# Sparse attention of the hybrid mixer by pairs of heads: scores, turns and outputs at every second place of a projection stream

## The chip, the core and the metric

The kernel runs on one core of one Trainium2 chip, as a single launch. The metric is the device time of one execution in microseconds; the median of three runs stands for a kernel. All data are fp32. Five instruction streams run side by side: TensorE (PE), VectorE (DVE), ScalarE (ACT), GpSimd (POOL) and SyncE (SP, which issues the DMAs).

## What is computed

The whole program is two layers of a mixed recurrent network followed by one block with a hybrid mixer and a mixture of 32 experts, for 256 tokens of width 1024. The change lies in the attention half of the hybrid mixer. Cut to what matters:

```python
DILATED_PAIRS = ((128, 1), (512, 4), (2048, 16))     # (window, dilation); 8 heads of width 64, 256 tokens

def hybrid_mixer(h, w_in, attn_norm_w, lb, hgrn_norm_w, w_out):
    proj = h @ w_in                                  # 1024 x 3584: qa ka va | qr fr ir gr
    ...
    for window, dil in DILATED_PAIRS:
        o, lse = dilated_causal_attention(qa, ka, va, window, dil)
        outs.append(o); lses.append(lse)
    wts = softmax(stack(lses), axis=0)
    o_a = einsum('nbsh,nbshd->bshd', wts, stack(outs))
    y_a = rms_norm_2(o_a, attn_norm_w)               # per head
    ...
    o_r = hgrn2_chunkwise(q_r, 1.0 - f, v_r, log(f)) # the recurrent half, 4 heads of width 128
    y_r = rms_norm_2(o_r, hgrn_norm_w) * silu(gr)
    return concatenate([y_a, y_r], axis=-1) @ w_out
```

The kernel folds the three windows into one softmax: each key gets the number of windows that contain it (0 to 3) as a factor (`cst["cnt"]`), and keys in none of them get -1e30 (`cst["neg"]`).

## The kernel before, in words

Every engine runs its stages in one fixed order: the first two layers, then `mixer2` (the hybrid mixer), then the experts (`moe_head`, `moe`). Engines wait for one another by named semaphore values: `P.mm(..., sig="at.s0")` signals, `wait_ge("at.s0")` waits, `free` says that a PSUM bank may be written again. Nothing is reordered at run time: an engine that waits holds up all that stands behind it.

In `mixer2` TensorE computes the projections `in2.*` one PSUM tile after another: a tile of `proj_p` is 16 matmuls 128x256, one of `proj_tok_p` 8 matmuls 128x512. The tiles take banks 0 to 3 in turn. The attention is a second stream *beside* this one: `att_p` is a generator, and with `P.pace = 1` each call of `P.tile` first runs it up to its next `yield`, a **step**. From the start of the stream the main tiles are

| step | 1 | 2 | 3 | 4 | 5 | 6 | 7 | 8 | 9 | 10 | 11 | 12 | 13 | 14 |
|---|---|---|---|---|---|---|---|---|---|---|---|---|---|---|
| tile after it | at.v0 | at.v1 | hg.f0 | hg.f2 | hg.q0 | hg.q2 | hg.v0 | hg.v1 | hg.g0 | hg.sc0 | hg.t0 | hg.sc1 | hg.t1 | hg.s0 |

(f, q, v, g are the gates, queries, values and output gate of the recurrent half; sc, t and s its scores, transposes and states.)

Before the change a step holds up to three things, each for another head (`k` counts the steps from 0):

- **scores** of head k: two matmuls with 64 rows (heads 2j and 2j+1 lie in rows 0 to 63 and 64 to 127 of `QA`, `KA`), into a side bank;
- **turns** of head k-1: three 128x128 transposes of the weights `PBS`, into a side bank, after `at.p{hd}`;
- **outputs** of head k-2: three matmuls from `PTB`, after ACT has copied the turned weights there (`free at.t{hd}`).

The side banks are 4 and 5, taken alternately by `side_tile`; taking one waits until its last user is free. In the code before, scores always find bank 5 (from the second on) and turns bank 4, so scores wait for DVE's reading of the scores one step earlier, and turns for ACT's copy one step earlier.

Between PE's parts, DVE scales and masks the scores (one instruction 128x384, which reads the bank), takes two maxima and negates them (`at.m`), ACT takes two exponentials (`at.e`), and DVE multiplies by the counts with a row sum (`at.p`).

DVE and ACT do their own parts of the side stream when it is **due**: `side_done(name)` records the current step, and an engine runs all side work that is due at step n just before it takes the main tile of step n. So ACT's order around step 5 is: the sigmoid parts of tile hg.f2 (`Exp`, then `Ln` and `Exp` of 512 elements), then the wait for `hg.ke` from DVE, then a `Ln` of 1024 elements, and only then, at `S.tile("hg.q0")`, the side work of step 5. Around step 7 it is: `Exp`, `Ln`, `Exp` for hg.q2, the wait for `hg.cum`, two `Exp` of 1024 elements, and then, at `S.tile("hg.v0")`, the side work of step 7. Around step 3 it is the copy of at.v1 and then the side work.

The loads of weights go through a ring of slots: SP issues the next load once PE has used the slot's former content. In the expert stage each job (two experts or four) loads units of 2 MB.

Of the kernel before, what the change touches and what calls it, by code (L numbers as in the profile page):

```python
# [9 lines left out]
ACT = mybir.ActivationFunctionType  # L10
AX = mybir.AxisListType.X
ADD, SUB, MUL, MAX, MIN = ALU.add, ALU.subtract, ALU.mult, ALU.max, ALU.min
# [609 lines left out]
def bc(ap, axis, n):  # L622

    u = ap.unsqueeze(axis)
    shape = list(u.shape)
    shape[axis] = n
    return u.to_broadcast(shape)
# [7 lines left out]
def build(nc, dram, out):  # L635
    ctx = ExitStack()
    with ctx:
# [7 lines left out]
        XS_ = sb("xs", 2 * D)  # L645
# [31 lines left out]
        cst, at = {}, 0  # L677
# [3 lines left out]
        at = sum(consts[n].shape[1] for n in list(consts)[:list(consts).index("gla")])  # L681
# [21 lines left out]
        OMU, NEG, at = {}, {}, 16  # L703
# [11 lines left out]
        def rsqrt_s(S, out, x, tmp, n):  # L715
            S.wait_ge(n + ".x")
            S.act(tmp, x, ACT.Ln)
            S.act(out, tmp, ACT.Exp, scale=-0.5)
            S.mark(n + ".e")

        def rsqrt_v(V, out, x, tmp, n):
            V.mark(n + ".x")
            V.wait_ge(n + ".e")
            V.tt(tmp, x, out, MUL)
            V.stt(tmp, tmp, -0.5, out, MUL, MUL)
            V.stt(out, tmp, 1.5, out, ADD, MUL)
# [17 lines left out]
        half64 = [slice(0, 64), slice(64, 128)]  # L744
# [1613 lines left out]
        QA, KA = MEMT[:, 0:4, :], MEMT[:, 4:8, :]  # L2358
        VA = AR.get(2, 512)
        PBS = [MX_[:, n * 384:(n + 1) * 384] for n in range(2)]  # L2360
        PTB = [MX_[:, n * 384:(n + 1) * 384] for n in range(2, 4)]
        AMX, ALS = SM[:, 124:140], SM[:, 140:156]
        OA = XS_[:, 0:1024].rearrange("p (i d) -> p i d", i=2)
        OSQ = XS_[:, 1024:2048].rearrange("p (h v) -> p h v", v=64)
        AR_, AR1, AR2 = SM[:, 156:172], SM[:, 172:188], SM[:, 188:204]
        SPLIT = ((0, slice(0, 128)), (1, slice(128, 384)))

        def att_p(P):

            oa = None  # L2370
            for k in range(10):
                if k < 8:
                    pr, j = half64[k % 2], k // 2
                    b = P.side_tile(f"at.s{k}")
                    P.wait_ge("free at.k2")
                    P.mm(b[:, 0:128], QA[pr, j, 0:128], KA[pr, j, 0:128], True, True)
                    P.mm(b[:, 128:384], QA[pr, j, 128:256], KA[pr, j, :], True, True, sig=f"at.s{k}")
                    P.side_done(f"at.s{k}")
                if 1 <= k < 9:
                    hd = k - 1  # L2380
                    b = P.side_tile(f"at.t{hd}")
                    P.wait_ge(f"at.p{hd}")
                    for q in range(3):
                        P.tr(b[:, q * 128:(q + 1) * 128], PBS[hd % 2][:, q * 128:(q + 1) * 128], ident,
                             sig=f"at.t{hd}" if q == 2 else None)
                    P.side_done(f"at.t{hd}")
                if k >= 2:
                    hd = k - 2
                    if hd == 0:
                        oa = [P.occupy(f"at.o{i}", 6 + i) for i in range(2)]  # L2390
                    vs = slice(hd * 64, hd * 64 + 64)
                    ptb = PTB[hd % 2]
                    P.wait_ge(f"free at.t{hd}", "free at.v1")
                    P.mm(oa[0][:, vs], ptb[:, 0:128], VA[:, 0, vs], True, True)
                    P.mm(oa[1][:, vs], ptb[:, 128:256], VA[:, 0, vs], True, False)
                    P.mm(oa[1][:, vs], ptb[:, 256:384], VA[:, 1, vs], False, True, sig=f"at.h{hd}")
                yield True
            for _ in range(2):
                yield True
            P.m.put("due at.sq", P.steps + 1)  # L2400
            yield True
            P.m.put("due at.o", P.steps + 1)
            for _ in range(2):
                yield True
            for i in range(2):
                b = P.side_tile(f"at.y{i}")
                P.wait_ge("at.on")
                for c in range(4):
                    P.tr(b[:, c * 128:(c + 1) * 128], OA[:, i, c * 128:(c + 1) * 128], ident,
                         sig=f"at.y{i}" if c == 3 else None)  # L2410
                P.side_done(f"at.y{i}")
            yield True

        def att_v(V):
            for hd in range(8):
                yield V.due_at(f"at.s{hd}")
                pb = PBS[hd % 2]
                b = V.got(f"at.s{hd}")
                if hd > 1:
                    V.wait_ge(f"at.t{hd - 2}")  # L2420
                V.stt(pb, b[:, 0:384], 0.125, cst["neg"], MUL, ADD)
                V.free(f"at.s{hd}")
                for i, s in SPLIT:
                    m = AMX[:, i * 8 + hd:i * 8 + hd + 1]
                    V.reduce(m, pb[:, s], MAX)
                    V.ts(m, m, -1.0, None, MUL, None)
                V.mark(f"at.m{hd}")
                V.wait_ge(f"at.e{hd}")
                for i, s in SPLIT:
                    V.stt(pb[:, s], pb[:, s], 1.0, cst["cnt"][:, s], MUL, MUL, accum=ALS[:, i * 8 + hd:i * 8 + hd + 1])  # L2430
                V.mark(f"at.p{hd}")
            yield V.due_at("at.o")
            V.recip(ALS, ALS)
            V.tt(AR2, ALS, ALS, MUL)
            V.wait_ge("at.sq")
            V.reduce(AR1, OSQ, ADD)
            V.tt(AR1, AR1, AR2, MUL)
            V.ts(AR1, AR1, 1.0 / 64, EPS, MUL, ADD)
            rsqrt_v(V, AR_, AR1, AR2, "at")
            V.tt(AR_, AR_, ALS, MUL)  # L2440
            for i in range(2):
                V.tt(OA[:, i, :].rearrange("p (h v) -> p h v", h=8), V.banks[6 + i].rearrange("p (h v) -> p h v", h=8),
                     bc(AR_[:, i * 8:i * 8 + 8], 2, 64), MUL)
                V.free(f"at.o{i}")
            V.mark("at.on")
            for i in range(2):
                yield V.due_at(f"at.y{i}")
                b = V.got(f"at.y{i}")
                V.tt(MIX[:, 0:4, i * 128:(i + 1) * 128], b.rearrange("p (c t) -> p c t", c=4),
                     bc(COL[:, coff["ang"]:coff["ang"] + 4], 2, 128), MUL)  # L2450
                V.free(f"at.y{i}")

        def att_s(S):
            for hd in range(8):
                yield S.due_at(f"at.s{hd}")
                pb = PBS[hd % 2]
                S.wait_ge(f"at.m{hd}")
                for i, s in SPLIT:
                    S.act(pb[:, s], pb[:, s], ACT.Exp, bias=AMX[:, i * 8 + hd:i * 8 + hd + 1])
                S.mark(f"at.e{hd}")  # L2460
                yield S.due_at(f"at.t{hd}")
                b = S.got(f"at.t{hd}")
                S.copy(PTB[hd % 2], b[:, 0:384])
                S.free(f"at.t{hd}")
            yield S.due_at("at.sq")
            S.wait_ge("at.h7")
            for i in range(2):
                S.act(OSQ[:, i * 8:i * 8 + 8, :], S.banks[6 + i].rearrange("p (h v) -> p h v", h=8), ACT.Square)
            S.mark("at.sq")
            yield S.due_at("at.o")  # L2470
            rsqrt_s(S, AR_, AR1, AR2, "at")
# [10 lines left out]
        def mixer2_p(P):  # L2482
# [4 lines left out]
            proj_p(P, "in2.0", "at.q", xn="m2")  # L2487
            proj_p(P, "in2.1", "at.k")
            P.beside(att_p(P))
            P.pace = 1  # L2490
            proj_tok_p(P, "in2.2", "at.v")
# [64 lines left out]
        def mixer2_s(S):  # L2556
# [12 lines left out]
            for n, dst in (("at.q", QA), ("at.k", KA)):  # L2569
                for j in (0, 2):  # L2570
                    b = S.tile(f"{n}{j}")
                    S.copy(dst[:, j:j + 2, :], pair(b))
                    S.free(f"{n}{j}")
            S.beside(att_s(S))
            S.wait_ge("hg.l")
            S.act(z0, z0, ACT.Exp)
# [59 lines left out]
        def mixer2_v(V):  # L2636
# [4 lines left out]
            root_v(V, "fin", out=RB1)  # L2641
            scaled_v(V, HT, HT, gain_of("final_g"), "fin", r=RB1, sig="h")
            V.beside(att_v(V))
            l0, l1 = COL[:, coff["lb"]:coff["lb"] + 4], COL[:, coff["lb"] + 4:coff["lb"] + 8]
            V.tt(lb, l0, l1, MAX)
# [108 lines left out]
        cnt, cum, st = NOV[:, 0, :], NOV[:, 1, :], NOV[:, 2, :]  # L2754
# [836 lines left out]
```

## Time and profile before

| | |
|---|---|
| median of 3 runs | 2265.56 us (2265.2 to 2265.84) |
| the profiled execution | 2268.09 us, span of its trace 2266.2 us |
| PE busy | 2127.8 us, 94% of the span |
| DVE, ACT, POOL busy | 619.3, 370.2, 125.3 us |
| DMA | 587.54 MB, mean 259 GB/s |
| mean granted TensorE clock | 0.974 of full |

The three medians agree within 0.6 us. The profile's times below are us from the start of the span. The side stream runs from 1144.7 (first scores) to about 1229. A matmul in fp32 is recorded as two instructions, a transpose as one; the busy time of PE overlaps from one instruction to the next, so the cost of a group is read from its start to the start of the next group.

### The profile page before, as it was taken

The numbers are of one execution on the slowest core, as the hardware profiler recorded it, in microseconds if no ns is written. First come the engines' busy times: TensorE is split into PE (matmuls) and PEld (weight loads), VectorE is DVE, ScalarE is ACT, GpSimd is POOL, SyncE is SP. The second block draws the span as 40 slices with busy tenths as digits, with TensorE's granted clock in tenths as the row PEclk, the third lists the DMA queues.
The fourth block names the chain that finished last, engine by engine and source line by source line (L and its number), as shares of the span: only waits on it lengthen the run. The fifth ranks groups of instructions, "written<-read, shape, count | busy, mean of one in ns | idle before, by whom it ended". The sixth has DMA issues, their size and how long they took to land.

```text
span 2266.2 us, 25809 instructions
## 1 busy us (share of the span) xinstructions
PE 2127.8 (94%) x10764; PEld 1413.8 (62%) x10764; DVE 619.3 (27%) x1229; ACT 370.2 (16%) x672; POOL 125.3 (6%) x186
## 2 busy tenths in 40 slices
PE   9999999999999999999999999996789999999765
PEld 6887788888888888888877753332334333433222
DVE  4344432334454224336225321000001010100001
ACT  4321122100014222000222320100001000001000
POOL 0113300000000000000000010100000000001000
PEclk9999999999999999999999999998889999999888
DMA  6321053444632445336533459999999999999997
GB/s 252 112 75 38 2 208 115 151 161 156 237 149 101 159 149 223 149 140 271 235 146 112 188 222 402 428 427 427 427 427 420 425 428 427 426 392 428 427 428 281
DMA packets 44427, 587.54 MB, mean 259 GB/s; under 512 B 5344, under 2 KB 5616, under 8 KB 9104
## 3 DMA queue, kind: packets, MB, share of 16 engines
q1 hardware_dynamic: 44304, 585.82, 63.8%
q8 instruction: 87, 1.43, 0.3%
q14 instruction: 36, 0.29, 0.0%
HBM read 584.75 MB, written 1.05 MB: 258 GB/s over the span
## 4 chain that ended last, share of the span: by engine, by line
PE 73%; DMA 24%; DVE 1%; ACT 1%; issue 1%; SPq 0%; PEld 0%; DVEq 0%; ACTq 0%; PEldq 0%
PE pb L410 72%; DMA kv<-in_gu 7%; DMA ring<-in_gu 6%; DMA ring<-in_dne 6%; DMA kv<-in_dne 2%; DMA arena<-in_dne 2%; PE pb L420 1%; DMA arena<-in_gu 1%; DVE arena L327 1%; ACT arena L371 0%; DVE arena L312 0%; DMA ht<-in_x 0%; DVE arena L321 0%; ACT arena L377 0%; DMA ring<-in_dn 0%
## 5 line engine op out<-in xcount | busy, mean ns | idle before, releaser
L410 PE MATMUL pb<-arena,ring 128*128 128x256 f32 (+1 forms) x2816 | 614.1, 380 | 4.9 <-ACT arena L371 2.0
L410 PEld LDWEIGHTS pb<-arena,ring 128*128 128x128 f32 (+1 forms) x2816 | 522.6, 188 | 89.4 <-issue 8.7
L410 PE MATMUL pb<-arena 128*128 128x256 f32 (+12 forms) x2644 | 491.3, 383 | 34.0 <-DMA ring<-in_dne 16.6
L410 PEld LDWEIGHTS pb<-arena 128*128 128x128 f32 (+5 forms) x2644 | 317.7, 168 | 194.1 <-issue 158.9
L410 PE MATMUL pb<-arena,cst 128*64 128x512 f32 (+6 forms) x1032 | 338.0, 617 | 58.6 <-DMA kv<-in_gu 40.8
L410 PE MATMUL pb<-ring,cst 128*64 128x512 f32 (+2 forms) x800 | 341.3, 628 | 0.0
L410 PEld LDWEIGHTS pb<-arena,cst 128*64 128x64 f32 (+4 forms) x1032 | 104.6, 140 | 265.4 <-issue 262.8
L410 PE MATMUL pb<-ring,arena 128*64 128x512 f32 (+2 forms) x480 | 192.1, 619 | 7.3 <-DMA arena<-in_dne 7.3
L377 ACT ACTIVATE arena<-pb 128x512 f32<-128x512 f32 (+4 forms) x123 | 68.7, 559 | 550.8 <-PE pb L420 420.4
L319 DVE TENSOR_SCALAR arena<-pb 128x512 f32<-128x512 f32 x30 | 20.8, 692 | 466.6 <-PE pb L410 466.6
L410 PEld LDWEIGHTS pb<-ring,cst 128*64 128x64 f32 (+2 forms) x800 | 100.0, 140 | 67.6 <-issue 67.6
L371 ACT ACTIVATE arena<-arena 128x512 f32<-128x512 f32 (+5 forms) x155 | 90.2, 582 | 300.6 <-DVE arena L327 271.1
L410 PE MATMUL pb<-kv,cst 128*64 128x512 f32 (+2 forms) x288 | 135.7, 627 | 0.0
L312 DVE TENSOR_TENSOR arena<-pb,arena 128x512 f32<-128x512 f32 (+5 forms) x114 | 60.7, 533 | 239.0 <-PE pb L410 230.4
L321 DVE TENSOR_SCALAR arena<-pb 128x512 f32<-128x512 f32 x30 | 20.7, 691 | 338.0 <-PE pb L410 338.0
L410 PEld LDWEIGHTS pb<-ring,arena 128*64 128x64 f32 (+2 forms) x480 | 62.3, 146 | 62.7 <-issue 62.7
L410 PE MATMUL pb<-arena,kv 128*128 128x256 f32 (+1 forms) x448 | 95.9, 380 | 1.2 <-ACT arena L377 1.2
L312 DVE TENSOR_TENSOR arena<-arena 128x512 f32<-128x512 f32 (+6 forms) x138 | 81.8, 593 | 39.4 <-ACT arena L371 29.0
L410 PEld LDWEIGHTS pb<-arena,kv 128*128 128x128 f32 (+1 forms) x448 | 80.8, 186 | 13.9 <-ACT arena L377 1.6
L377 ACT ACTIVATE memt<-pb 128x512 f32<-128x512 f32 x36 | 21.5, 597 | 377.7 <-PE pb L410 377.5
L327 DVE SCALAR_TENSOR_TENSOR arena<-arena 128x512 f32<-128x512 f32 (+4 forms) x94 | 67.2, 715 | 18.9 <-ACT arena L371 11.0
L410 PEld LDWEIGHTS pb<-arena,xs 128*128 128x128 f32 (+2 forms) x540 | 63.2, 190 | 10.1 <-issue 8.7
(145 smaller groups left out, 1472.3 us busy)
## 6 DMA issues: line engine op xcount, KB each, us to landing
arena<-in_gu SPq DMA_DIRECT2D x60, 2048.0 KB, 18.6
ring<-in_gu SPq DMA_DIRECT2D x50, 2048.0 KB, 19.4
arena<-in_dne SPq DMA_DIRECT2D x33, 2048.0 KB, 19.4
ring<-in_dne SPq DMA_DIRECT2D x21, 2048.0 KB, 19.4
kv<-in_gu SPq DMA_DIRECT2D x18, 2048.0 KB, 19.4
ring<-in_up SPq DMA_DIRECT2D x13, 2048.0 KB, 7.8
ring<-in_wkv SPq DMA_DIRECT2D x8, 2048.0 KB, 7.8
ring<-in_dn SPq DMA_DIRECT2D x8, 2048.0 KB, 7.6
```

Source lines behind the costliest of these rows:

```text
L312: self.e.tensor_tensor(out, a, b, op).then_inc(self.sem, 1)
L319: self.e.tensor_scalar(out, a, s1, None, op0).then_inc(self.sem, 1)
L321: self.e.tensor_scalar(out, a, s1, s2, op0, op1).then_inc(self.sem, 1)
L327: self.e.scalar_tensor_tensor(out, a, s, b, op0, op1, accum_out=accum).then_inc(self.sem, 1)
L371: self.e.activation(out, a, func, bias=bias, scale=scale, accum_out=accum).then_inc(self.sem, 1)
L377: self.e.activation(out, a, ACT.Copy).then_inc(self.sem, 1)
L410: r = self.e.matmul(out, lhsT, rhs, start=start, stop=stop, skip_group_check=True)
L420: r = self.e.transpose(out, a, ident)
```

## The change

The head-by-head pipeline becomes one of pairs. Scores of both heads of a pair are issued together, alternating between the two row halves; the turns of a pair are issued together, and so are its outputs. All this stands at the odd steps only: scores of pair j at step 2j+1, turns of pair j at step 2j+3 ahead of the scores of pair j+1, outputs of pair j at step 2j+5 between the two. The outputs of the last pair stand at step 10. DVE and ACT do both heads of a pair together, and `PTB` has four buffers where it had two.

```diff
+        PTB += [XS_[:, 1024 + n * 384:1408 + n * 384] for n in range(2)]
...
-            for k in range(10):
-                if k < 8:
-                    pr, j = half64[k % 2], k // 2
-                    b = P.side_tile(f"at.s{k}")
-                    P.wait_ge("free at.k2")
+            def scores(j):
+                bs = [P.side_tile(f"at.s{2 * j + n}") for n in range(2)]
+                P.wait_ge("free at.k2")
+                for b, pr in zip(bs, half64):
                     P.mm(b[:, 0:128], QA[pr, j, 0:128], KA[pr, j, 0:128], True, True)
-                    P.mm(b[:, 128:384], QA[pr, j, 128:256], KA[pr, j, :], True, True, sig=f"at.s{k}")
-                    P.side_done(f"at.s{k}")
-                if 1 <= k < 9:
-                    hd = k - 1
+                for n, (b, pr) in enumerate(zip(bs, half64)):
+                    P.mm(b[:, 128:384], QA[pr, j, 128:256], KA[pr, j, :], True, True, sig=f"at.s{2 * j + n}")
+                P.side_done(f"at.s{2 * j + 1}")
+
+            def turns(j):
+                for hd in (2 * j, 2 * j + 1):
                     b = P.side_tile(f"at.t{hd}")
                     P.wait_ge(f"at.p{hd}")
...
-                if k >= 2:
-                    hd = k - 2
...
+            def heads(j):
+                if j == 0:
+                    oa.update({i: P.occupy(f"at.o{i}", 6 + i) for i in range(2)})
+                for hd in (2 * j, 2 * j + 1):
                     vs = slice(hd * 64, hd * 64 + 64)
-                    ptb = PTB[hd % 2]
+                    ptb = PTB[hd % 4]
                     P.wait_ge(f"free at.t{hd}", "free at.v1")
...
+            for j in range(5):
+                if j >= 1:
+                    turns(j - 1)
+                if j >= 2:
+                    heads(j - 2)
+                if j < 4:
+                    scores(j)
+                yield True
+                if j == 4:
+                    heads(3)
                 yield True
...
         def att_s(S):
-            for hd in range(8):
-                yield S.due_at(f"at.s{hd}")
...
+            for j in range(4):
+                heads = (2 * j, 2 * j + 1)
+                yield S.due_at(f"at.s{2 * j + 1}")
+                for hd in heads:
+                    S.wait_ge(f"at.m{hd}")
...
+                yield S.due_at(f"at.t{2 * j + 1}")
+                for hd in heads:
+                    b = S.got(f"at.t{hd}")
+                    S.copy(PTB[hd % 4], b[:, 0:384])
+                    S.free(f"at.t{hd}")
```

In `att_v` the waits and instructions are the same, with the masks and maxima of both heads first and the two multiplications of each head after them.

## Rows read from the trace of the kernel before

**Rows 1.** The page: the chain that ended last, by engine.

```profile
PE 73%; DMA 24%; DVE 1%; ACT 1%; issue 1%; SPq 0%; PEld 0%; DVEq 0%; ACTq 0%; PEldq 0%
```

**Rows 2.** The chain in order of time, around 1370: start, us, what.

```profile
1370.23 7.04 PE pb L410 x32
1377.66 17.38 DMA kv<-in_gu
```

**Rows 3.** Busy time by stretch: PE, PEld, DVE, ACT, POOL, granted clock, DMA share, GB/s.

```profile
1310.00:1378.00 68.00, 65.71 (x330) 29.48 (x332) 12.45 (x37) 8.40 (x15) 8.48 (x17) 0.97 0.70 275
1378.00:1591.00 213.00, 181.70 (x896) 69.84 (x892) 21.19 (x38) 19.26 (x33) 15.23 (x32) 0.94 1.01 427
```

**Rows 4.** Timeline of PE at step 7: scores, turns, outputs, next tile.

```profile
1196.41 0.92 PE L410 MATMUL pb<-memt 64*128 64x128 f32 x4
1197.26 0.55 PE L420 MATMUL pb<-cst,arena 128*128 128x128 f32 x3
1197.64 0.78 PE L410 MATMUL pb<-arena 128*128 128x64 f32 x6
1198.26 7.09 PE L410 MATMUL pb<-ring,arena 128*128 128x512 f32 x16
```

**Rows 5.** Timeline of PE: matmuls in alternate row halves, and what follows them.

```profile
1087.71 2.00 PE L410 MATMUL pb<-arena 64*128 64x256 f32 x16
1089.64 4.58 PE L410 MATMUL pb<-arena,ring 128*128 128x256 f32 x20
```

**Rows 6.** Timeline of ACT at step 2: tile at.v0, then the copy of a turn.

```profile
1152.69 0.60 ACT L377 ACTIVATE arena<-pb 128x512 f32<-128x512 f32 x1 [4.00 <-PE pb L410]
1154.02 0.49 ACT L377 ACTIVATE arena<-pb 128x384 f32<-128x384 f32 x1 [0.73 <-PE pb L420]
```

**Rows 7.** Timeline of all engines at step 2, DVE: the first and the last work on one head.

```profile
1153.54 0.56 DVE L327 SCALAR_TENSOR_TENSOR arena<-pb,cst 128x384 f32<-128x384 f32 x1 [4.05 <-PE pb L410]
...
1156.59 0.42 DVE L327 SCALAR_TENSOR_TENSOR arena<-arena,cst 128x256 f32<-128x256 f32 x1
```

**Rows 8.** Timeline of all engines at step 5, PE and ACT.

```profile
1178.59 0.92 PE L410 MATMUL pb<-memt 64*128 64x128 f32 x4
...
1178.70 0.60 ACT L371 ACTIVATE arena<-pb 128x512 f32<-128x512 f32 x1 [2.84 <-PE pb L410]
...
1182.02 1.06 ACT L371 ACTIVATE arena<-arena 128x1024 f32<-128x1024 f32 x1 [1.39 <-DVE arena L321]
...
1183.16 0.49 ACT L377 ACTIVATE arena<-pb 128x384 f32<-128x384 f32 x1
```

**Rows 9.** Timeline of ACT at step 7.

```profile
1197.14 3.47 ACT L371 ACTIVATE arena<-arena 128x512 f32<-128x512 f32 x4
1200.70 0.49 ACT L377 ACTIVATE arena<-pb 128x384 f32<-128x384 f32 x1
```

**Rows 10.** Timeline of PE at steps 10 to 14: outputs and hg.sc0, hg.t0, hg.s0.

```profile
1221.96 1.72 PE L410 MATMUL pb<-arena 128*128 128x64 f32 x14
1223.52 0.60 PE L420 MATMUL pb<-cst,arena 128*128 128x128 f32 x4
...
1226.86 1.12 PE L410 MATMUL pb<-arena 32*128 32x128 f32 x8 [0.97 <-DVE arena L312]
```

**Rows 11.** Timeline of ACT at steps 11 to 13: copies of hg.t0 and hg.t1.

```profile
1224.17 0.60 ACT L377 ACTIVATE arena<-pb 128x512 f32<-128x512 f32 x1
...
1226.12 0.60 ACT L377 ACTIVATE arena<-pb 128x512 f32<-128x512 f32 x1
```

**Rows 12.** Timeline of PE at tile hg.f0, a whole tile of a projection.

```profile
1162.63 7.12 PE L410 MATMUL pb<-arena,ring 128*128 128x256 f32 x32
```

**Rows 13.** Busy time by stretch, as in Rows 3: short stretches, earlier stages.

```profile
701.40:704.90 3.50, 2.41 (x11) 1.51 (x9) 0.91 (x3) 3.12 (x6) 0.00 (x0) 0.99 0.00 0
704.90:708.30 3.40, 3.07 (x8) 2.61 (x9) 3.26 (x5) 1.30 (x4) 0.00 (x0) 0.51 0.00 0
1111.10:1114.50 3.40, 2.18 (x11) 1.57 (x9) 2.65 (x6) 0.86 (x3) 0.00 (x0) 1.00 1.00 429
```

More of the change, by code:

```diff
@@ L2368, in att_p @@
         def att_p(P):
-            oa = None
-            for k in range(10):
-                if k < 8:
-                    pr, j = half64[k % 2], k // 2
-                    b = P.side_tile(f"at.s{k}")
-                    P.wait_ge("free at.k2")
-                    P.mm(b[:, 0:128], QA[pr, j, 0:128], KA[pr, j, 0:128], True, True)
-                    P.mm(b[:, 128:384], QA[pr, j, 128:256], KA[pr, j, :], True, True, sig=f"at.s{k}")
-                    P.side_done(f"at.s{k}")
-                if 1 <= k < 9:
-                    hd = k - 1
+            oa = {}
+            def scores(j):
+                bs = [P.side_tile(f"at.s{2 * j + n}") for n in range(2)]
+                P.wait_ge("free at.k2")
+                for b, pr in zip(bs, half64):
+                    P.mm(b[:, 0:128], QA[pr, j, 0:128], KA[pr, j, 0:128], True, True)
+                for n, (b, pr) in enumerate(zip(bs, half64)):
[3 more added lines that the diff above has]
+                for hd in (2 * j, 2 * j + 1):
                     b = P.side_tile(f"at.t{hd}")
@@ L2385, in att_p @@
                              sig=f"at.t{hd}" if q == 2 else None)
-                    P.side_done(f"at.t{hd}")
-                if k >= 2:
-                    hd = k - 2
-                    if hd == 0:
-                        oa = [P.occupy(f"at.o{i}", 6 + i) for i in range(2)]
+                P.side_done(f"at.t{2 * j + 1}")
+            def heads(j):
+                if j == 0:
+                    oa.update({i: P.occupy(f"at.o{i}", 6 + i) for i in range(2)})
+                for hd in (2 * j, 2 * j + 1):
                     vs = slice(hd * 64, hd * 64 + 64)
-                    ptb = PTB[hd % 2]
+                    ptb = PTB[hd % 4]
                     P.wait_ge(f"free at.t{hd}", "free at.v1")
@@ L2415, in att_v @@
             for hd in range(8):
-                yield V.due_at(f"at.s{hd}")
                 pb = PBS[hd % 2]
+                if hd % 2 == 0:
+                    yield V.due_at(f"at.s{hd + 1}")
                 b = V.got(f"at.s{hd}")
@@ L2427, in att_v @@
                 V.mark(f"at.m{hd}")
[L2428 to L2431, printed above, removed]
+                if hd % 2 == 0:
+                    continue
+                for h1 in (hd - 1, hd):
+                    V.wait_ge(f"at.e{h1}")
+                    for i, s in SPLIT:
+                        pb = PBS[h1 % 2][:, s]
+                        V.stt(pb, pb, 1.0, cst["cnt"][:, s], MUL, MUL, accum=ALS[:, i * 8 + h1:i * 8 + h1 + 1])
+                    V.mark(f"at.p{h1}")
             yield V.due_at("at.o")
@@ L2453, in att_s @@
         def att_s(S):
-            for hd in range(8):
-                yield S.due_at(f"at.s{hd}")
[L2456 to L2464, printed above, removed]
+            for j in range(4):
[3 more added lines that the diff above has]
+                    S.wait_ge(f"at.m{hd}")
+                    for i, s in SPLIT:
+                        pb = PBS[hd % 2][:, s]
+                        S.act(pb, pb, ACT.Exp, bias=AMX[:, i * 8 + hd:i * 8 + hd + 1])
+                    S.mark(f"at.e{hd}")
+                yield S.due_at(f"at.t{2 * j + 1}")
[3 more added lines that the diff above has]
+                    S.free(f"at.t{hd}")
             yield S.due_at("at.sq")
```

## The prediction

> **What bounds the kernel now.** I read the chain that ended last first: 73% of it is PE, 24% DMA [rows 1]. In order of time it is almost only PE up to 1377, and at 1377.66 it passes to loads of expert weights that follow one another [rows 2]. The busy times by stretch say the same: from 1378 on the DMA engines are fully busy (share 1.01, 427 GB/s), in the 68 us before only 0.70 of the time [rows 3]. The changed place, 1144 to 1229, lies in the PE part. Here PE never waits for the side stream: a step with all three parts is followed at once by its projection tile [rows 4]. So each microsecond that PE gains or loses here moves all that comes after. That holds for the DMA part too: its loads are issued when PE gives a slot back, and no load in the 0.70 stretch fills the engines, so the stream of loads starts as much later as PE does. I count 1:1.
>
> **What PE's work costs, before and after.** From start to start at step 7 [rows 4]: scores of one head 0.85 us (1196.41 to 1197.26), turns 0.38, outputs 0.62; 1.85 a head, 14.8 us for eight.
>
> Scores of a pair: four matmuls, recorded as eight instructions, four with 128 columns and four with 256. The trace has no such group, but it has 16 instructions 64x256 in alternate row halves: 1.93 us from start to start, 0.121 each [rows 5], where a 128-row instruction with 256 columns takes 7.12/32 = 0.2225 [rows 12]. So the halves do overlap, to nearly twice the rate. A single head's 0.85 against 2 x 0.11 + 2 x 0.2225 = 0.67 leaves 0.18 for filling and changing over. For the pair: low bound 4 x 0.06 + 4 x 0.121 = 0.72, all at double rate with no edge; high bound twice 0.85 = 1.70, no overlap and nothing saved. I take 1.10: the 256-column ones at 0.121, the 128-column ones near their full 0.11 since each still loads 128 columns of weights, and an edge of 0.18. Turns of a pair: 2 x 0.33 + 0.05 = 0.71. Outputs: 12 instructions at 0.62/6, 1.24. Together 3.05 a pair, 12.2 for four: **2.6 us less** than 14.8. With the bounds of the scores it is 4.1 less to 0.2 less.
>
> The Trainium skill (TensorE: Matmul & The Clock Gate, Part 3, The mechanism) says that matmuls in different row groups run at the same time, and the halves above agree in part (1.8 times the rate). By that rule alone a pair's scores would take one head's 0.85, and the sum below would be 1.0 us smaller.
>
> **The wait that the new order puts in.** The side banks are two. `scores(j)` takes both before its first matmul, and the users before it are the two turns of the *same* step. So PE, standing at step 3, 5 or 7, must wait until ACT has copied both turns out; behind it stand the scores and the next projection tile. Before, the copy had a whole tile (7.12 us, [rows 12]) of cover; now it has only the outputs in between (1.24 at steps 5 and 7, nothing at step 3). And ACT does the copies only after its work on the main tile that has just ended. Let T be the end of the main tile ahead of the step, which is also the start of the step.
>
> - *Step 3.* ACT copies at.v1 first (0.60, starting 0.11 after T, as [rows 6]: 1152.69 against 1152.58). The turns' results come 0.55 after their start; copies of 0.49 from T+0.73, T+1.25, done at T+1.74. With 0.14 for the signal PE starts the scores at T+1.88, without the wait at T+0.71: **1.17**.
> - *Step 5.* T = 1178.59 in the old trace. ACT does tile hg.f2 (0.60 and 1.29), waits for DVE (`hg.ke`; 1.39 idle), does its `Ln` of 1.06, and starts the one copy of this step at 1183.16, T+4.57 [rows 8]. None of what stands ahead of it depends on the new order, so the two copies end at T+5.56 and the scores start at T+5.70. PE has turns and outputs until T+1.95: **3.75**.
> - *Step 7.* T = 1196.41. ACT runs 3.47 us in four `Ln` and `Exp` with no gap, so `hg.cum` isn't late, and the copy starts at 1200.70, T+4.29 [rows 9]. Two copies end at T+5.28, scores at T+5.42: **3.47**. DVE's scan ahead of `hg.cum` follows tile hg.q0; it still has the whole tile hg.q2 (7.12) and ACT's work on that (1.9) ahead of the wait, only the side work of step 6 (1.85) is gone from between.
>
> Sum of the waits **8.4 us**. Their bounds: nothing (rival 4), and 9.9 with one more ACT instruction of 0.49 ahead of each two copies.
>
> Other waits stay covered. From the first DVE instruction to the last one head takes 3.5 us [rows 7], a pair some 5.5; between scores and turns of a pair lie two tiles, 14 us. Steps 9 and 10 have no scores, so their turns and outputs wait for nothing.
>
> *Step 10* now has outputs of two heads, 0.62 more. The idle 0.97 ahead of hg.s0 [rows 10] looks like cover, but ACT's copy of hg.t0 starts at 1224.17, right after PE's transposes end (1223.52 + 0.60), and the copy of hg.t1 ends at 1226.72, 0.14 ahead of hg.s0 [rows 11]. So this 0.62, which is inside the 12.2, is not hidden. I count it in full.
>
> PE's sum: -2.6 + 8.4 = **+5.8 us**.
>
> **The clock.** An idle stretch can also cost speed. At 701.4 to 704.9 PE was busy 2.41 of 3.5 us, a good part of it in matmuls of 4 rows, and at 704.9 to 708.3 it was granted 0.51, the 1.2 GHz level, with 8 matmuls where 3.40/0.2225 = 15 would fit; that costs 1.7 us. With 2.18 of 3.40 busy at 1111 it kept 1.00, the 2.4 GHz level [rows 13]. The two waits of 3.5 to 3.75 leave PE far emptier than either. I expect a fall after each, of 0.8 to 1.7 us, part of it lying in the wait itself: **+2.4** for both, bounds 0 and 3.5. The wait of 1.17 costs no clock.
>
> The Trainium skill (same page, Part 1, What's actually happening) says the clock is throttled by default and only activity releases it, which speaks against this change; the row at 704.9 agrees.
>
> Total +5.8 + 2.4 = **+8.2**: 2265.56 + 8.2 = 2273.8 us, 0.36% slower. The profiled execution was 2268.09 (span 2266.2), 2.5 above the median; such an execution of the changed kernel would be near 2276.3, its span 2274.4.
>
> **The rivals.**
>
> 1. *Waits and clock, as forecast*: 2273.8, range 2271.5 to 2276. Chance 0.55.
> 2. *Waits without the clock*: the turns and outputs around the waits keep it at 2.4 GHz, as at 1111. 2265.56 + 5.8 = 2271.4. Chance 0.2.
> 3. *The row halves don't overlap*, so the change doesn't do what it says: one bank after another, 1.33 + 0.18 = 1.5 to 1.7 for a pair, that is 1.6 to 2.4 more. 2273.8 + 2 = 2275.8. For it: the two heads start with their 128-column matmuls, which no row shows alternating; against it: [rows 5]. Chance 0.1.
> 4. *The copies come in time* (the other side): ACT takes the copies before its work on the finished tile, at T+0.7 at steps 5 and 7. Then the outputs cover them but for 0.1 to 0.6. It decides once the copies end before T+1.8, against T+5.56 by my reading of the order. Only the gain is left, less about 1 us at step 3: 2265.56 - 1.5 = 2264.1, no difference that can be measured. Chance 0.08.
> 5. *The delay is swallowed later*: 8 us less idle for PE in the expert stage, where it has 31 of 213 us idle [rows 3], since the DMA stream sets the end. It would need loads that are issued at the old time whatever PE does. 2265.6 to 2268. Chance 0.07.
>
> **How the numbers follow.** What a measurement of this kernel can tell from no change is about 0.2%, 4.5 us, so the border is at 2270.1. Rival 1 and 3 are above it, rival 2 mostly (its own spread is about 2 us; I give 0.15 of its 0.2), 4 and 5 within. Slower 0.81, same 0.17, faster 0.02. The range of 8 in 10 takes in rival 2 and 3, leaving out 4, 5 and the ends: 2268.5 to 2277.5.
>
> **What the profile after would show.** PE idle ahead of its memt matmuls (the scores) three times, about 1.2, 3.7 and 3.5 us, released by ACT's copies of 128x384; nothing of this ahead of the turns. Groups of eight memt instructions of about 1.1 us from start to start, four times. ACT copies in twos. Steps 2, 4, 6 and 8 without any side work. A granted clock of about 0.5 for some 3 us after step 5 and after step 7. The chain passing from PE to DMA near 1386 instead of 1377.66. It would make me wrong if ACT's copies stood ahead of its main tile's work, if the release of a bank came otherwise than through those copies, or if the DMA stream started at its old time.

## The result and the profile after

The changed kernel takes 2278.91 us (median of 4 runs, 2277.48 to 2280.86) against 2265.70 beside it: 1.0059 times, 95% interval 1.0041 to 1.0076, so 13.2 us slower. The forecast was 2273.8 with a range up to 2277.5. The direction was right, the size and the range were not. One execution of a later kernel (four side banks, late outputs, split biases) took 2674.55 us at a mean granted clock of 0.84; it does not count in that kernel's ratio, and without it the median is 2262.99 instead of 2263.24.

The profiled execution of the changed kernel took 2278.09 us, its span is 2276.3. PE around the side stream, from the timeline of the kernel after (start, us, engine and operation, in brackets the idle time before and what ended it):

```profile
1142.14 0.93 PE L410 MATMUL pb<-memt 64*128 64x128 f32 x8 [0.78 <-ACT memt L377]
...
1156.83 0.82 PE L420 MATMUL pb<-cst,arena 128*128 128x128 f32 x6
1158.94 0.93 PE L410 MATMUL pb<-memt 64*128 64x128 f32 x8 [1.29 <-ACT arena L377]
...
1173.71 0.82 PE L420 MATMUL pb<-cst,arena 128*128 128x128 f32 x6
1174.37 1.45 PE L410 MATMUL pb<-arena 128*128 128x64 f32 x12
1179.59 1.02 PE L410 MATMUL pb<-memt 64*128 64x128 f32 x8 [3.77 <-ACT xs L377]
1180.54 15.63 PE L410 MATMUL pb<-arena,ring 128*128 128x256 f32 x64
...
1196.66 1.45 PE L410 MATMUL pb<-arena,xs 128*128 128x64 f32 x12
1201.66 1.66 PE L410 MATMUL pb<-memt 64*128 64x128 f32 x8 [3.56 <-ACT arena L377]
1203.25 16.14 PE L410 MATMUL pb<-ring,arena 128*128 128x512 f32 x32
...
1233.69 1.12 PE L410 MATMUL pb<-arena 32*128 32x128 f32 x8 [1.40 <-ACT arena L377]
1234.75 8.86 PE L410 MATMUL pb<-arena,kv 128*128 128x256 f32 x32
```

The `memt` rows are the scores, now eight instructions for a pair. The three new waits stand ahead of them and nowhere else, 1.29, 3.77 and 3.56 us; before the change PE had none here [rows 4]. ACT just ahead of the second one, in the timeline of ACT after, shows what it waited for: the `Ln` of 1024 elements behind `hg.ke`, then the two copies:

```profile
1177.22 1.06 ACT L371 ACTIVATE arena<-arena 128x1024 f32<-128x1024 f32 x1 [1.39 <-DVE arena L321]
1178.37 1.07 ACT L377 ACTIVATE xs<-pb 128x384 f32<-128x384 f32 x2
```

The copies start 4.66 us after the tile's end at 1173.71 (before 4.57, [rows 8]). Behind the long waits the two tiles between two steps, 14.1 us at full clock, take 15.6 and 16.1. Busy time by stretch of the kernel after (PE, PEld, DVE, ACT, POOL, granted clock, DMA share, GB/s):

```profile
1176.00:1179.60 3.60, 0.01 (x2) 0.04 (x2) 1.12 (x3) 2.04 (x3) 0.00 (x0) 1.00 0.92 387
1180.30:1183.70 3.40, 3.40 (x10) 2.54 (x9) 2.78 (x9) 0.91 (x2) 0.00 (x0) 0.50 0.41 149
...
1200.80:1207.60 6.80, 5.93 (x13) 2.81 (x14) 3.77 (x13) 2.23 (x6) 0.00 (x0) 0.50 0.31 129
1234.90:1238.30 3.40, 3.40 (x9) 2.65 (x10) 2.56 (x9) 0.43 (x2) 0.00 (x0) 0.50 0.02 5
1347.50:1350.90 3.40, 3.40 (x10) 0.77 (x8) 0.00 (x0) 0.00 (x0) 0.00 (x0) 0.51 1.02 439
```

So the clock is at its 1.2 GHz level (a **fall** in what follows) behind step 5, for twice as long behind step 7, once behind hg.s0 (ahead of which PE idled 1.40 us), and in the expert stage at 1347.5. The chain passes to the DMA stream 8.5 us later than in the first profile of before [rows 2]:

```profile
1378.73 7.04 PE pb L410 x32
...
1386.17 17.28 DMA kv<-in_gu
```

The forecast had 1386 for this, but the hit is luck: the two profiles do not start the side stream at the same time, and from the first scores on the change costs 11.1 us up to this point (244.0 against 233.0).

Profiles of one kernel differ in the stages ahead of and behind the change, by where the clock falls. The first profile of before fell at 128.0 and 704.9, the profile after at 1112.0 instead, and the first began its scores 2.6 us later. At 1112.0 to 1115.4 the profile after was granted 0.50, and so was the second profile of before at 1112.7 to 1116.1, both behind 2.00 us of idle. Behind the same idle, which lies in the third line of [rows 13], the first profile of before kept 1.00. The instructions there are the same, so they alone do not decide whether a fall comes. So I compare stretches, from the starts in the PE timelines (e0 is the first job of the expert stage, and 32x512 its matmuls with 32 rows and 512 columns; the DMA stream begins where the chain passes to DMA):

| kernel | first scores | to hg.s0 | hg.s0 to first 32x512 of e0 | that to the DMA stream | from there to the span's end |
|---|---|---|---|---|---|
| before, two profiles | 1144.7, 1142.6 | 82.2, 82.2 | 92.7, 92.7 | 58.1, 56.4 | 888.5, 889.8 |
| after, two profiles | 1142.1, 1144.7 | 91.5, 91.5 | 94.4, 94.3 | 58.1, 58.1 | 890.1, 894.8 |

Up to hg.s0 the change costs 9.4 us, both times; 1.7 are added right behind it, both times; the rest of the 13 lies further behind. That rest is badly known: the interval of the ratio makes the whole 9.3 to 17.2 us, and the execution of the second profile of after took 2285.24 us, 4.7 above its median.

### The profile page after: what moved, and what is told of

It is laid out like the page before. It is cut to its first block, busy times and chain, and to the rows that moved or that the text cites. A ratio compares the mean times of both kernels' runs of the same rounds, so it can differ in the third digit from the quotient of the medians.

```text
span 2276.3 us, 25805 instructions
## 1 busy us (share of the span) xinstructions
PE 2130.8 (94%) x10764; PEld 1415.4 (62%) x10764; DVE 619.5 (27%) x1229; ACT 370.2 (16%) x672; POOL 125.2 (6%) x186
## 4 chain that ended last, share of the span: by engine, by line
PE 71%; DMA 25%; ACT 2%; DVE 1%; issue 0%; SPq 0%; ACTq 0%; DVEq 0%
PE pb L410 70%; DMA ring<-in_gu 8%; DMA kv<-in_gu 8%; DMA ring<-in_dne 5%; DMA kv<-in_dne 3%; DMA arena<-in_gu 1%; DMA arena<-in_dne 1%; PE pb L420 1%; ACT arena L371 1%; DVE arena L327 1%; ACT arena L377 0%; DVE arena L321 0%; DMA ht<-in_x 0%; ACT xs L371 0%; DVE arena L312 0%
## 5 line engine op out<-in xcount | busy, mean ns | idle before, releaser
L410 PE MATMUL pb<-arena 128*128 128x256 f32 (+12 forms) x2620 | 486.4, 383 | 31.5 <-DMA ring<-in_dne 17.3
L410 PEld LDWEIGHTS pb<-arena 128*128 128x128 f32 (+5 forms) x2620 | 312.9, 167 | 192.7 <-issue 157.4
```

What stands on the lines that cost most here:

```text
L410: r = self.e.matmul(out, lhsT, rhs, start=start, stop=stop, skip_group_check=True)
```

## The experiments

Each was timed in five rounds beside the kernel before (medians of 2265.4 to 2266.8); ratios are to that, with 95% intervals. Spare matmuls are 128x256 with a result that nobody uses, about 0.44 us each.

### Four side banks

```diff
-        k = self.second[self.j % 2]
+        k = self.second[self.j % len(self.second)]
...
             P.pace = 1
+            P.main, P.second = [0, 1], [2, 3, 4, 5]
...
             proj_tok_p(P, "in2.5", "hg.v")
+            P.main, P.second, P.j = [0, 1, 2, 3], [4, 5], 0
```

> The changed kernel with four side banks (2 to 5) and two main banks (0, 1) during steps 1 to 8, so that scores no longer take the banks of the turns of the same step. Theory A (the wait for ACT's copies of the turns and the clock falls behind it are the whole loss): no wait ahead of the scores at steps 3, 5 and 7, no fall of the granted clock near them, PE's side work 3.6 us less than before the change (0.86 instead of 1.70 for the scores of a pair in the profile after), so about 2262, 3 to 4 us faster than the kernel before. Theory B (the loss comes from DVE and ACT doing two heads at a time, which makes the main tiles late): the time stays near 2279. Theory C (two main banks are too few, a new wait of projection tiles for their banks takes the place): idle of PE ahead of 128x256 or 128x512 projection matmuls, and a time between 2264 and 2275.

2265.17 us, ratio 0.9995 (0.9986 to 1.0003). What PE waited for from 1140 to 1240, in this kernel:

```profile
PE pb L410 <- ACT arena L377: 1.4, 1, 1.4
PE pb L410 <- ACT memt L377: 0.8, 1, 0.8
```

The three waits are gone and no main tile waits for a bank. From scores to hg.s0 it is 78.21 us, 3.95 less than before the change and 13.3 less than after it. So the banks are the cause, and B and C fall. But the time didn't follow: of 3.95 us about 1 is left. Busy time by stretch of this kernel shows two places behind that took it:

```profile
1142.00:1216.00 74.00, 74.00 (x330) 52.81 (x327) 29.26 (x90) 25.87 (x46) 0.00 (x0) 1.00 0.39 145
1220.40:1223.80 3.40, 3.40 (x11) 2.64 (x10) 2.63 (x9) 0.43 (x2) 0.00 (x0) 0.51 0.03 5
1333.10:1339.90 6.80, 6.80 (x18) 1.63 (x16) 0.00 (x0) 0.18 (x1) 0.00 (x0) 0.50 1.01 431
```

PE is busy all through 1142 to 1216 at full clock; then it is slow behind hg.s0 and again, for twice as long, in job e0 of the experts.

### The same, one head after the other

```diff
-                for b, pr in zip(bs, half64):
-                    P.mm(b[:, 0:128], QA[pr, j, 0:128], KA[pr, j, 0:128], True, True)
                 for n, (b, pr) in enumerate(zip(bs, half64)):
+                    P.mm(b[:, 0:128], QA[pr, j, 0:128], KA[pr, j, 0:128], True, True)
                     P.mm(b[:, 128:384], QA[pr, j, 128:256], KA[pr, j, :], True, True, ...)
```

> As the kernel with four side banks, but the four score matmuls of a pair are issued one head after the other instead of in alternate row halves. Theory A (alternate halves run at the same time, 0.86 us for a pair as for one head): a pair now takes about 1.5 us, 4 x 0.65 = 2.6 us more than the kernel with four side banks, about 2264.5 to 2265. Theory B (the gain of the pair comes from fewer changes between kinds of matmul, not from the halves): 0.9 to 1.0 us for a pair and a time within 0.5 us of the kernel with four side banks.

2266.73 us, ratio 1.0000 (0.9991 to 1.0009). A pair's scores in the PE timeline, from their start to the next tile's:

```profile
1173.63 0.93 PE L410 MATMUL pb<-memt 64*128 64x128 f32 x8
1174.49 14.08 PE L410 MATMUL pb<-arena,ring 128*128 128x256 f32 x64
```

0.86 us, as with alternate halves, and 78.24 us to hg.s0. Both theories missed. The time is 1.6 us above that of the kernel with four side banks by the medians, but the intervals overlap and up to hg.s0 it is 0.03. Theory B's reason doesn't hold: one head alone took 0.85 [rows 4], so the two heads do run at the same time, in either order of the kernel's text. What puts them side by side, the trace doesn't show. The Trainium skill (TensorE: Matmul & The Clock Gate, Part 3, The mechanism) says that matmuls keep strict program order in start and end; by that the second head could start here only with the last instruction of the first, and the pair would take some 1.4 to 1.5 us, an estimate from the 0.85 of one head and the 0.2225 of a 256-column instruction. The measured 0.86 speaks against it for different row halves. Its rule that such matmuls run at the same time holds.

### Spare matmuls in the two long waits

```diff
+                if j > 1:
+                    P.warm(f"at.w{j}", ident, cst["tri"], 7, bank=P.main[P.i % 4])
                 bs = [P.side_tile(f"at.s{2 * j + n}") for n in range(2)]
```

> The changed kernel with 7 spare matmuls of 128x256 (3.1 us, result unused) between the outputs and the scores at steps 5 and 7, where PE otherwise waits 3.77 and 3.56 us. Theory A (the falls of the clock behind the two waits cost about 4 to 6 us by themselves): the scores start at the same distance from the end of the main tile ahead, the granted clock stays at 1.00 up to 1225, and the time is 4 to 6 us under that of the changed kernel, 2273 to 2275. Theory B (the lower clock is only seen while PE idles and costs nothing): 2278 to 2280, unchanged.

2271.75 us, ratio 1.0026 (1.0016 to 1.0036): 7 us less than the changed kernel, by work added. To hg.s0 87.05 instead of 91.55. The scores start at the same distance, now mostly filled:

```profile
1176.12 3.24 PE L410 MATMUL pb<-cst 128*128 128x256 f32 x14
1180.06 0.93 PE L410 MATMUL pb<-memt 64*128 64x128 f32 x8 [0.70 <-ACT xs L377]
1180.92 14.08 PE L410 MATMUL pb<-arena,ring 128*128 128x256 f32 x64
```

Theory A holds, and what it expected was still too little: the lower clock costs 4.5 us up to hg.s0, and the fall behind hg.s0 (1.7) is gone too, though PE still idles 1.40 us ahead of it.

### ACT's copies ahead of its other waits

```diff
+            S.reach("hg.q0")
             S.wait_ge("hg.ke")
...
+            S.reach("hg.v0")
             S.wait_ge("hg.cum")
```

> The changed kernel with two lines more in ACT's stream: ACT takes the side work of step 5 ahead of its wait for hg.ke and the side work of step 7 ahead of its wait for hg.cum, so that the copies of the turns stand right behind the sigmoid of the main tile. Theory A (the length of the wait is set by ACT's main work standing ahead of the copies): the copies start at T+2.1 instead of T+4.6 and T+4.3, the waits fall to about 1.3 us each, the clock falls behind them mostly go, and the time is 2270 to 2272. Theory B (the wait is for something else than those copies, such as DVE's reading of the score banks): waits and time stay as in the changed kernel, 2279; the 2 us of exponentials now standing ahead of the Ln may then even add to it.

2267.60 us, ratio 1.0011 (0.9999 to 1.0023), better than expected. Both long waits fall to 1.32 us, the clock stays, 82.36 us to hg.s0:

```profile
1177.49 0.93 PE L410 MATMUL pb<-memt 64*128 64x128 f32 x8 [1.32 <-ACT xs L377]
1178.35 14.08 PE L410 MATMUL pb<-arena,ring 128*128 128x256 f32 x64
...
1195.69 0.93 PE L410 MATMUL pb<-memt 64*128 64x128 f32 x8 [1.32 <-ACT arena L377]
```

So it is ACT's order that made the waits long. Three waits of 1.3 us eat up all that the pairs save.

### Outputs of the last pair at step 12

Four side banks as above, and

```diff
-                if j == 4:
-                    heads(3)
                 yield True
-            for _ in range(2):
+            for n in range(2):
+                if n:
+                    heads(3)
                 yield True
```

> The kernel with four side banks, and the outputs of the last pair moved from step 10 (ahead of hg.sc0) to step 12 (between hg.t0 and hg.sc1). Theory A (at step 10 they delay ACT's copy of hg.t0 and with it hg.s0, which also leaves PE idle for 1.40 us and costs a fall of the clock): hg.s0 comes 4.9 us after the end of tile hg.g0 as before the change, not 5.5, the idle ahead of it is about 0.8, no fall behind it; 0.6 + 1.6 us less than with four side banks alone, 2262 to 2263.5, the fastest so far. Theory B (hg.s0 hangs on DVE's work on the score tiles): hg.s0 stays at 5.5 us and the time near 2265.

2265.76 us beside 2266.77, ratio 0.9993 (0.9983 to 1.0003). Up to hg.s0 theory A is right to the tenth: 77.62 us, 4.96 from the end of tile hg.g0, idle 0.80, no fall there. Yet the gain is again not to be seen at the end. In the expert stage this profile has 59.7 us from the first 32x512 to the DMA stream, as with four side banks alone (59.8), instead of the 56.4 to 58.1 of before:

```profile
1330.20:1337.00 6.80, 6.80 (x17) 1.87 (x18) 0.00 (x0) 0.37 (x1) 0.00 (x0) 0.50 1.00 429
```

Ahead of that stand the four bias matmuls of job e0 with 32 rows, 3.69 us in a row (1326.57). What the late outputs had gained over four side banks alone went even later: the DMA stream starts 2.4 us earlier (1371.34 against 1373.70), but the last stretch takes 892.1 us against 889.5. Such last stretches, 888 to 895 us in the profiles, also differ between two profiles of one kernel.

### Both kernels again, and a plain delay

The changed kernel and the kernel before, unchanged:

> The changed kernel once more, for a second profile and more times. Theory A (the last 2 us of the 13.2 are chance in where the clock falls meet the stages behind): a median between 2276.5 and 2279, again 91 to 92 us from the first scores to hg.s0, with falls of the clock behind steps 5 and 7 that may differ in length. Theory B (a steady further cost outside the stage): 2279 again, and the same extra time at one place of the expert stage in both profiles.

> The kernel before once more, for a second profile. 82.2 us from the first scores to hg.s0, as it has no falls of the clock there. The time is 2265.4 as before. Theory A of the run above says that its start of the scores and its expert stage differ from the first profile by 1 to 3 us each.

The kernel before with 22 spare matmuls ahead of `scores` at step 5, and with 11:

```diff
+                    if k == 4:
+                        P.warm("at.w", ident, cst["tri"], 22, bank=P.main[P.i % 4])
                     b = P.side_tile(f"at.s{k}")
```

> The kernel before with 22 spare matmuls of 128x256 (result unused) ahead of the scores at step 5: PE is 22 x 0.445 = 9.8 us busier at the changed place, with no wait and no fall of the clock. Theory A (all that PE loses here passes to the end, 1:1): 2265.4 + 9.8 = 2275.2. Theory B (the expert stage, bound by DMA, swallows part of it): 2268 to 2273.

> The kernel before with 11 spare matmuls of 128x256 ahead of the scores at step 5, half of the delay tried before: 11 x 0.445 = 4.9 us, of which the larger one passed 9.4 to hg.s0 for 9.8. Theory A (a delay passes 1:1, and on top of it comes what the clock does at the two weak places behind): 4.7 at hg.s0 and 4.7 to 8.1 at the end, 2270 to 2274. Theory B (the stages behind stretch a delay in proportion, 13 for 9.4): 2272 with no further fall of the clock.

| run | us | ratio (interval) | to hg.s0 |
|---|---|---|---|
| after again | 2280.57 | 1.0062 (1.0048 to 1.0076) | 91.50 |
| before again | 2266.12 | 1.0002 (0.9993 to 1.0011) | 82.15 |
| 22 spare matmuls | 2279.86 | 1.0063 (1.0049 to 1.0076) | 91.65 |
| 11 spare matmuls | 2273.20 | 1.0030 (1.0018 to 1.0041) | 86.90 |

The second profile of each kernel gives the same time up to hg.s0 as the first; the median of the changed kernel came 1.6 us above what theory A of that run allowed. The plain delay of 9.5 us up to hg.s0 costs as much as the change does, 13 to 14 us. So past hg.s0 it doesn't seem to matter how the time was lost; what came on top of the 9.4, some 4 us, needs neither the new order of ACT and DVE nor the buffers in `XS_`. Neither theory of the larger delay foresaw more than 1:1. In its profile two falls stand at the same two places as in the profile after; the second of them the first profile of before has too (1339.7, 3.4 us), the second profile of before not:

```profile
1235.00:1238.40 3.40, 3.40 (x10) 2.58 (x9) 2.63 (x9) 0.43 (x2) 0.00 (x0) 0.51 0.00 0
1347.70:1351.10 3.40, 3.40 (x10) 0.77 (x8) 0.00 (x0) 0.10 (x1) 0.00 (x0) 0.50 0.99 424
```

The smaller one passes 4.75 to hg.s0 and 6.8 (4.1 to 9.3) to the end, in the range that theory A of it gave. The interval takes in 1:1.

### The delay at two other places

`m2.w` (ahead of the mixer's first projection) with 30 instead of 4 matmuls, and `mo.w2` (ahead of the experts) with 27 instead of 5.

> The kernel before with 22 more spare matmuls of 128x256 just ahead of the expert stage, behind hg.s0: a delay of 22 x 0.445 less 0.5 of idle, 9.3 us, at full clock. Theory A (a delay of 9.4 us up to hg.s0 costs 13 at the end because of what the clock does in the places between hg.s0 and the expert stage): this one costs about 9.3 to 11, 2275 to 2277. Theory B (the expert stage itself takes longer when it starts later): 13 here too, 2279 to 2280.

> The kernel before with 26 more spare matmuls of 128x256 at the start of the hybrid mixer, ahead of its first projection, where PE waits 2.0 us: a delay of 26 x 0.445 less 2.0, 9.6 us, at full clock and with no change to the side stream. Theory A and B of the run above both expect 13 here (2279 to 2280), as in the runs with 9.4 us at hg.s0; if it is 9.6 instead (2275 to 2276), the stretching belongs to the place in the attention stream.

Ahead of the experts: 2277.72 us, ratio 1.0042 (1.0028 to 1.0056); the stretch from the last group of matmuls out of `xs` and `small` to the first 32x512 grew from 23.4 to 32.1, 8.7 us. Ahead of the mixer: 2277.06, ratio 1.0036 (1.0023 to 1.0048). Here the delay was smaller than expected: the first scores came at 1152.9 against 1144.7 in the first profile of before, which had the same falls up to there, so 8.2 us and not 9.6. By the ratios that is 9.5 and 8.2 us at the end, by the medians 11.3 and 10.6, for 8.7 and 8.2: nearer to 1:1 than the 13 to 14 for 9.5, and neither profile has the fall behind hg.s0. But both fell for 6.8 us at the biases of e0 (59.7 and 59.8 us to the DMA stream), and the interval of the first overlaps that of the 22 spare matmuls, while that of the second ends just below it and is for a smaller delay. So the difference is likely, not proven.

### The bias matmuls in two pairs

The four bias matmuls of job e0 as two and two: with four side banks and late outputs; in the kernel before; and in the changed kernel with two spare matmuls ahead of hg.s0.

```diff
-        def biases_p(P):
+        def biases_p(P, part):
...
-            for i, half in TURNS:
+            for i, half in TURNS[2 * part:2 * part + 2]:
...
                     if at == 0:
+                        biases_p(P, 1)
                         sorted_p(P)
...
-                    biases_p(P)
+                    biases_p(P, 0)
```

`biases_p(P, 0)` runs first, where all four stood; `biases_p(P, 1)` behind the turned activations. In these three the second pair reads `BDOWN` after the turned activations were written over it, so they add other numbers than the biases for tokens 128 to 255; the instructions and their sizes are the same.

> The kernel with four side banks and late outputs, with one edit in the expert stage: the four bias matmuls of job e0 (32 rows, 512 columns, 3.7 us in a row) are issued in two pairs, one where all four stood and one behind the turned activations of the same job. No work is added. Theory A (the row of 32-row matmuls brings a fall of the clock, 6.8 us long in the profile of the kernel with late outputs, and that ate the gain): no fall there, expert stage 1.7 to 3.4 us shorter, 2262 to 2264. Theory B (the gain is lost elsewhere): 2265 to 2266, unchanged.

> The kernel before with the same edit of the bias matmuls alone, as a control. Theory A: before the change the fall at the biases is 0 to 3.4 us long in the two profiles, so at most 1 us faster, 2264.5 to 2265.5. Theory B (the split itself costs, by one more change of the kind of matmul): 0 to 0.5 us slower.

> The changed kernel with the split bias matmuls and 2 spare matmuls of 128x256 in PE's wait ahead of hg.s0. Theory A (the step from 9.4 us at hg.s0 to 13 at the end is two falls of the clock, 1.7 us each, behind hg.s0 and behind the biases): both gone, 70.0 instead of 71.7 us from hg.s0 on, and 2275 to 2276. Theory B (the rest is lost in the DMA stream): 2278 to 2280.

The first took 2263.24 us, ratio 0.9985 (0.9975 to 0.9994); the second, the control, 2265.81, ratio 0.9999 (0.9990 to 1.0008). So the edit seems to have paid where the pairs' gain had been lost (without it the ratio was 0.9993), and did nothing that can be seen for the kernel before; but the intervals with and without it overlap (0.9975 to 0.9994, 0.9983 to 1.0003), so that it paid is not shown. And the profile of the first does not show theory A's reason: it has two falls of 3.4 us, at 1331.2 and at 1348.2, and 59.3 us to the DMA stream, hardly less than the 59.7 without the split. The profiled execution took 2266.21 us, 3 above the median, so the usual one may look otherwise. The third missed: 2279.77 us, ratio 1.0053 (1.0039 to 1.0067). Its idle ahead of hg.s0 is 0.35 and no fall stands behind it, but one came at 1278.3, and hg.s0 to the first 32x512 is 94.3 us as in the changed kernel. With one idle place filled, a fall stood at another.

### The best version

Four side banks, late outputs, and the split with the first pair ahead of the second half of the up projection, where `BDOWN` is whole:

```diff
                 def first():
+                    if at == 0:
+                        biases_p(P, 0)
...
-                    biases_p(P)
+                    biases_p(P, 1)
```

> The changed kernel with four side banks, the outputs of the last pair at step 12, and the four bias matmuls of job e0 in two pairs, one pair moved to ahead of the second half of the up projection, the other where all four stood. Nothing is added or left out. Theory A (4.5 us less up to hg.s0 and no long fall of the clock at the biases): 2262 to 2264, faster than both kernels. Theory B (the stages behind give the gain back): 2265 to 2266.

2262.32 us beside 2266.45, ratio 0.9976 (0.9965 to 0.9988): 0.24% faster than the kernel before and 0.8% faster than the changed one. It has a fall between hg.s0 and the expert stage (at 1264.7; 94.35 us from hg.s0 to the first 32x512, as in the changed kernel), and none from there to the DMA stream:

```profile
1264.70:1268.10 3.40, 3.40 (x10) 2.69 (x9) 0.00 (x0) 0.00 (x0) 0.00 (x0) 0.50 1.03 352
1316.00:1374.00 58.00, 56.94 (x274) 22.08 (x276) 7.86 (x14) 6.64 (x11) 8.10 (x17) 1.00 0.74 293
```

## Why the prediction was right in kind and wrong in size

| term | forecast | measured | by |
|---|---|---|---|
| PE's work for the side stream, step 10 in it | -2.6 | -3.95 | four side banks, 78.21 against 82.16 to hg.s0 |
| waits at steps 3, 5, 7 | 1.17 + 3.75 + 3.47 = 8.4 | 1.29 + 3.77 + 3.56 = 8.6 | profile after |
| clock, up to hg.s0 | 2.4 in all | 4.7 (91.55 - 78.21 - 8.62) | 4.5 with spare matmuls in the waits |
| clock right behind hg.s0 | 0 | 1.7 | 94.4 against 92.7, two profiles each |
| further behind | 0 (1:1) | about 2 | the rest of 13.2, whose interval is 9.3 to 17.2 |

**The work.** I took 1.10 us for a pair's scores; it is 0.86, the value by the rule of the Trainium skill that I had set aside, and that makes 1.0 of the 1.35 us of difference. The 128-column instructions overlap fully too. Rival 3 (no overlap) is refuted. This error went the other way than those below and hid a part of them: with the scores priced right the sum would have been 7.2 and further off.

**The waits.** This step held to 0.2 us in sum, place by place, as did the count of what stands ahead of ACT's copies. With four banks or with earlier copies the waits go as the mechanism says. Rival 4 is the kernel with early copies: it needs two more lines in ACT's stream, and even so its copies start only at T+2.2 (1176.27 against 1174.06), not in time.

**The clock** is the step that failed. I let each long wait cost one fall, shorter than the one at 704.9, part of it hidden in the wait. The first wait brought one of 3.4 us, the second one of 6.8, of which PE worked 5.93; half of 3.40 and of 5.93 is 4.7 us, where my term for both was 2.4. Nothing of the first lay in the wait (granted 1.00 up to 1179.6), and 0.87 us of the second. Rival 2 is refuted. A third fall, behind hg.s0 (1.7), had no term at all. PE idles 1.40 us ahead of it, more than before (0.97), since my step 10 now holds two heads' outputs. But this idle time alone does not bring the fall: of six profiles with 1.40 us four have it (both of after, and the two kernels with four side banks and the last outputs still at step 10) and two have not (spare matmuls in the waits, early copies); with 0.97 or less it stands in one of eleven, that of the 22 spare matmuls.

**"I count 1:1"** failed as well. What is lost in the attention stream comes out as 13 to 14 for 9.4, for a plain delay too; what is saved there comes out as about 1 for 4. The intervals of the second runs of the changed kernel and of the 22 spare matmuls, from 10.9 and 11.1 us on, exclude 9.4; that of the first run only just includes it, and the smaller delay and those at the two other places allow 1:1. Rival 5, the delay swallowed later, is refuted: the stages behind added to it. Shown is the fall behind hg.s0, in both profiles after and with the plain delay. What stays open: about 2 us of the 13.2, between chance in where the clock falls in the expert stage (its last stretch varies from 888 to 895 us over the profiles) and a steady cost; and whether and how the split biases let the saving through, since one profile with them still had its falls there and the best version's none. I did not find what decides whether a place gets a fall.

## What to carry to other kernels

When work of two steps is put together, write down for each buffer who used it last: here the order "turns, then scores" was harmless until both needed the same two banks in one step, and then the longest chain of the *other* engine's main work became PE's wait. The cheap cures are to take the buffers apart (two main banks were enough) or to move the consumer's release ahead of its long waits. And a forecast for a PE-bound kernel needs the clock as a term at every place behind the change where PE idles or works on few rows, not only at the new wait; judge a saving by the end time, since a later fall can take it.

## What the runs showed of the hardware

- Two chains of 64-row matmuls in different row halves ran at the same time, 0.86 us for both and 0.85 for one, written in turns and written one after the other.
- Waits of 3.77 and 3.56 us with PE idle were followed by 3.4 and 6.8 us at the 1.2 GHz level, in both profiles; filled with spare matmuls they were not, and the kernel with *more* work was 7 us faster.
- PE busy without a gap was slowed too: behind four matmuls of 32 rows and 512 columns (3.69 us in a row, busy all the time) the clock was at its lower level for 0, 3.4 or 6.8 us, depending on the execution. That these matmuls are the reason is not shown. Busy time by stretch of the kernel after, just ahead of its fall at 1347.5:

```profile
1344.10:1347.50 3.40, 3.40 (x12) 1.22 (x11) 1.14 (x2) 0.37 (x1) 0.00 (x0) 1.00 1.00 328
```
- The same instructions at the same place can have a fall in one execution and none in another: behind 2.00 us of idle at the start of the mixer (1112.7 in the second profile of before, granted 0.50) and not in the first.
